# A conditioned decoder block on eight cores: x tiles in blocks and on another queue, the first squares summed on PE, the end by token halves

## The chip, the cores and the metric

The kernel runs on all eight cores of one Trainium2 chip. Each core computes one of eight sequences (4096 tokens of width 1024) with the same weights; the cores exchange nothing. The metric is the device time of the slowest core in microseconds (us). Engines are named as in the profile: PE is TensorE, DVE VectorE, ACT ScalarE, POOL GpSimd and SP SyncE. POOL and SP compute next to nothing here; they issue transfers, POOL on a queue whose descriptors are made in software (q0), SP on one with hardware descriptors (q1).

## The reference

The residual stream `x` (f32) goes through two feed-forward blocks (FFN) with a mixing block between, each behind an RMS norm that a conditioning vector `c` scales and shifts, and through a last such norm. Cut to what the change touches:

```python
D_MODEL = 1024; SEQ = 4096; D_FF = 2816
def rmsnorm(x, g):
    y = x * lax.rsqrt(jnp.mean(x * x, axis=-1, keepdims=True) + EPS)
    return y * g
def ada_rmsnorm(x, g, shift, scale):
    return rmsnorm(x, g) * (1.0 + scale) + shift
def swiglu_ffn(h, w_in, w_out):
    gate, up = jnp.split(h @ w_in, 2, axis=-1)
    return (jax.nn.silu(gate) * up) @ w_out

mod = silu(c) @ w_mod + b_mod                 # sh1, sc1, gt1, ... 9 vectors
h = ada_rmsnorm(x, g_ffn1, sh1, sc1)
x = x + 0.5 * gt1 * swiglu_ffn(h, w_ffn1_in, w_ffn1_out)
h = ada_rmsnorm(x, g_mix, sh2, sc2)
x = x + gt2 * (concat(conv_group(h), rglru_group(h)) @ w_out)
h = ada_rmsnorm(x, g_ffn2, sh3, sc3)
x = x + 0.5 * gt3 * swiglu_ffn(h, w_ffn2_in, w_ffn2_out)
return ada_rmsnorm(x, g_final, f_shift, f_scale)
```

## The kernel before

**Tiles.** The 4096 tokens of a core are eight tiles of T = 512. A tile is held with features on the partitions: eight blocks (`fc` 0 to 7) of 128 features by 512 tokens, f32, 2 MB in all, in one of four slots `xs` (sb_x). Its normalised copy in bf16 lies in one of three slots `hbs` (sb_hb). The hidden layer of an FFN (22 blocks of 128 by 512, bf16) is `hidA` or `hidB`.

**FFN.** The weights of an FFN are 33 slabs of 128 by 2048, read through a ring of five slots `fslots` (sb_fs). Slab `cg` below 22 holds 8 gate and 8 up blocks of one hidden block: 16 matmuls of 512 columns into two PSUM banks, then ACT takes the Silu of the gate bank into `sgf`, DVE multiplies with the up bank into the hidden layer (`evict`). The last 11 slabs are the output projection: for each of eight output blocks `oc` 22 matmuls into one bank, and DVE adds it, times the gate vector, into x (`oevict`). In its first use a slab comes as f32 from `w1` by POOL, which casts it on the way (`load_cast`), and SP writes it back in bf16 (`write_back`) for the later uses, which SP loads.

**Order of the work.** FFN 1 runs over pairs of tiles, (2, 3), (4, 5), (0, 1), then 6 and 7; the mixer and FFN 2 run over single tiles. The work is written as streams (generators), and `run_streams` interleaves them when the program is built, by a cost model. So each engine has a fixed list of instructions, which it carries out in order, with waits on semaphores between engines. A DMA's semaphore rises by 16.

**Head.** The modulation vectors come from 88 slabs of `wmod` (128 by 1024, f32, 512 KB). SP loads the first 16 at once (`modl_gen`) into buffers that are free then (sb_rs, sb_cs, sb_hidA, sb_hidB, sb_hb); DVE multiplies each with silu(c) and sums it (one SCALAR_TENSOR_TENSOR of 128x1024 into sb_junk, `mod_gen`), and every fourth frees a quarter of the first norm's scale and shift. Meanwhile POOL loads the first tile in one transfer (`xl_gen`, line 766), ACT squares its blocks, DVE adds the squares (`stats`, `accum`), one matmul with ones (`total`) sums over the partitions, ACT makes the reciprocal root by Ln and Exp (`rstd_ops`, sb_rstdm), and DVE and ACT apply it (`apply`). `head_gen` lets the first weight slab go when the ninth modulation slab is done, then the second x tile (one transfer on POOL, gated on the twelfth), then the others when the fifteenth is done.

**Between.** `o_gen` squares and sums x behind FFN 2 of a tile, applies the last norm and stores y in eight blocks on POOL, each with its own semaphore `s_y[fc]` (line 1284). The slot is then given to a later tile, whose eight block loads (`xload`) each wait for the store of the same block. In a pair or a mixer tile the statistics go by `stats` as above.

**End.** For the last tile the same: 8 x 22 matmuls of 512 columns, each output block squared and added as it comes, then the ones-matmul, Ln and Exp, eight DVE and ACT passes and eight stores.

## Time and profile before

| | us |
|---|---|
| median of three runs | 2373.75 |
| the three runs | 2369.35, 2373.75, 2509.9 |
| the profiled execution | 2375.25 |
| its span (first to last instruction), slowest core 7 | 2373.7 |
| the cores' spans | 2348.4 to 2373.7 |
| PE busy | 2249.8 (95%) |
| DVE busy | 1324.7 (56%) |
| ACT busy | 956.6 (40%) |
| POOL busy | 287.0 (12%) |

The profile is of one execution, of the slowest core. Busy time is what an engine spent inside instructions, its share is of the span. Matmuls overlap in the record (one of 512 columns is shown as some 380 ns while the next starts 217 ns after it), so a matmul's pace is read from the length of a run of them by their number. "Idle before" names what an engine waited for last. The granted clock is a share of TensorE's full 2.4 GHz; its lower level, 0.50, is 1.2 GHz.

### The profile page before, as it was taken

The page shows a single profiled execution, that of the slowest core. Times are in us where ns is not written, and L with a number is a line of the kernel's source. Part 1 is how long each engine was busy: PE and PEld are TensorE (multiplying, and loading weights), DVE is VectorE, ACT ScalarE, POOL GpSimd, SP SyncE. Part 2 cuts the span into 40 slices and gives each one's busy share as a digit, 9 for nine tenths or more (in the row PEclk, how much of TensorE's full clock was granted, in tenths as well). Part 3 has the DMA queues.
Part 4 walks back from the last instruction along what each step waited for, and adds up shares of the span by engine and source line. Part 5 has one row for each costly group of instructions (what it writes and reads, how often), then busy time and mean ns, then how long its engine had stood idle before and what let it go on. Part 6 is the DMA issues. An engine that isn't in the chain of part 4 may idle for free.

```text
span 2373.7 us, 34088 instructions; the slowest of 8 cores (2348.4 to 2373.7 us)
## 1 busy us (share of the span) xinstructions
PE 2249.8 (95%) x10864; PEld 1006.1 (42%) x10864; DVE 1324.7 (56%) x2131; ACT 956.6 (40%) x1473; POOL 287.0 (12%) x552
## 2 busy tenths in 40 slices
PE   1999998998999899899999999999999999999995
PEld 0444443443444344344444444444444444444442
DVE  5323225524433485674776476487487588477522
ACT  3313213303110533553565536436536556454512
POOL 0011110020000110201110120111111111120000
PEclk9999999999999999999999999999999999999998
DMA  9899798899866685654665665556456566564452
GB/s 258 189 232 215 194 206 214 214 212 243 214 187 164 191 223 170 190 167 141 194 207 158 207 200 191 154 171 227 153 178 214 160 171 222 158 186 138 151 177 89
DMA packets 122704, 446.86 MB, mean 188 GB/s; under 512 B 18864, under 2 KB 19248, under 8 KB 121520
## 3 DMA queue, kind: packets, MB, share of 16 engines
q1 hardware_dynamic: 90864, 330.44, 44.7%
q0 software_dynamic: 31664, 114.23, 21.5%
q8 instruction: 91, 1.49, 0.3%
q14 instruction: 85, 0.70, 0.1%
HBM read 426.87 MB, written 71.30 MB: 210 GB/s over the span
## 4 chain that ended last, share of the span: by engine, by line
PE 85%; DMA 8%; issue 2%; DVE 2%; ACT 2%; POOL 1%; SPq 0%; DVEq 0%; ACTq 0%; POOLq 0%
PE ps L457 83%; DMA sb_x<-x 2%; PE ps L1097 2%; DMA sb_cs<-wmod 2%; DMA sb_fs<-b 1%; DMA sb_fs<-w 1%; DMA sb_hidB<-wmod 1%; DMA sb_cs<-bm 1%; DVE sb_rstdm L441 1%; DMA x<-sb_x 0%; SPq L417 0%; POOL sb_urep L1087 0%; ACT sb_hb L434 0%; POOL sb_x L417 0%; ACT sb_ntmp L434 0%
## 5 line engine op out<-in xcount | busy, mean ns | idle before, releaser
L457 PE MATMUL ps<-sb_hb,sb_fs 128*128 128x512 bf16 x5632 | 1245.6, 382 | 35.5 <-DMA sb_fs<-w 14.2
L457 PEld LDWEIGHTS ps<-sb_hb,sb_fs 128*128 128x128 bf16 x5632 | 553.9, 98 | 711.8 <-issue 62.5
L457 PE MATMUL ps<-sb_hidA,sb_fs 128*128 128x512 bf16 x2288 | 505.7, 379 | 0.8 <-DVE sb_hidA L441 0.8
L434 ACT ACTIVATE sb_sgf<-ps 128x512 f32<-128x512 f32 x352 | 206.5, 593 | 406.8 <-PE ps L457 364.3
L457 PEld LDWEIGHTS ps<-sb_hidA,sb_fs 128*128 128x128 bf16 x2288 | 223.9, 98 | 269.6 <-issue 1.3
L441 DVE TENSOR_TENSOR sb_hidA<-ps,sb_sgf 128x512 bf16<-128x512 f32 x286 | 195.4, 688 | 227.1 <-PE ps L457 161.4
L457 PE MATMUL ps<-sb_hb,sb_cs 128*128 128x512 bf16 x992 | 224.2, 379 | 4.5 <-DMA sb_cs<-bm 3.4
L1087 POOL DMA_DIRECT2D sb_urep<-sb_ub x256 | 131.0, 520 | 694.5 <-PE ps L457 435.6
L437 DVE SCALAR_TENSOR_TENSOR sb_x<-ps,sb_gth,sb_x 128x512 f32<-128x512 f32 x128 | 96.0, 750 | 174.8 <-PE ps L457 174.4
L434 ACT ACT_TABLE_LOAD x102 | 130.9, 1283 | 154.4 <-PE ps L457 134.1
L437 DVE SCALAR_TENSOR_TENSOR sb_ux<-sb_ub,sb_vecs,sb_ux 128x512 f32<-128x512 bf16 x240 | 179.7, 749 | 10.0 <-DVE sb_ux L437 0.9
L434 ACT ACTIVATE sb_ntmp<-sb_x 128x512 f32<-128x512 f32 x168 | 103.6, 627 | 197.7 <-DVE sb_x L437 110.7
L441 DVE TENSOR_TENSOR sb_rstdm<-sb_rstdm,sb_ntmp 128x512 f32<-128x512 f32 x144 | 99.3, 689 | 131.5 <-ACT sb_ntmp L434 127.5
L437 DVE SCALAR_TENSOR_TENSOR sb_ntmp<-sb_x,sb_gs,sb_rstdm 128x512 f32<-128x512 f32 x192 | 137.8, 748 | 50.0 <-ACT sb_rstdm L434 41.7
L434 ACT ACTIVATE sb_hb<-sb_ntmp,sb_modv 128x512 bf16<-128x512 f32 x192 | 133.1, 720 | 43.1 <-DVE sb_ntmp L437 42.7
L457 PEld LDWEIGHTS ps<-sb_hb,sb_cs 128*128 128x128 bf16 x992 | 96.5, 98 | 122.3 <-issue 7.6
L457 PE MATMUL ps<-sb_hb,sb_rs 128*128 128x512 bf16 x544 | 128.8, 381 | 0.6 <-DVE sb_gy L437 0.4
L457 PE MATMUL ps<-sb_hidB,sb_fs 128*128 128x512 bf16 x528 | 117.9, 379 | 0.0
L441 DVE TENSOR_TENSOR sb_hidB<-ps,sb_sgf 128x512 bf16<-128x512 f32 x66 | 45.6, 691 | 109.5 <-PE ps L457 106.0
L417 POOL DMA_DIRECT2D y<-sb_x x64 | 35.0, 547 | 521.3 <-ACT sb_sgf L434 198.0
L437 DVE SCALAR_TENSOR_TENSOR sb_x<-ps,sb_modv,sb_x 128x512 f32<-128x512 f32 x64 | 47.9, 749 | 74.4 <-PE ps L457 74.3
L457 PEld LDWEIGHTS ps<-sb_hb,sb_rs 128*128 128x128 bf16 x544 | 53.4, 99 | 66.7 <-issue 4.1
(104 smaller groups left out, 1338.6 us busy)
## 6 DMA issues: line engine op xcount, KB each, us to landing
sb_fs<-b SPq DMA_DIRECT2D x396, 512.0 KB, 4.4
sb_cs<-bm SPq DMA_DIRECT2D x78, 512.0 KB, 4.1
sb_x<-x POOLq DMA_DIRECT2D x96, 256.0 KB, 7.9
sb_cs<-wmod SPq DMA_DIRECT2D x46, 512.0 KB, 12.6
sb_rs<-bm SPq DMA_DIRECT2D x34, 512.0 KB, 5.0
sb_fs<-w POOLq DMA_DIRECT2D x33, 512.0 KB, 9.9
b<-sb_fs SPq DMA_DIRECT2D x33, 512.0 KB, 8.8
b<-w POOLq DMA_DIRECT2D x33, 512.0 KB, 10.3
```

What stands on the lines that cost most here:

```text
L417: return Op(eng, lambda h: [h.dma_start(out=out_ap, in_=in_ap)], reads, writes, dma=sem, nbytes=nbytes)
L434: return Op(ACT, lambda h: [h.activation(out=out, in_=in_, func=func, **kw)], reads, writes, cost, tset)
L437: return Op(DVE, lambda h: [h.scalar_tensor_tensor(out=out, in0=in0, scalar=scalar, in1=in1, op0=op0, op1=op1)], reads, writes, cost)
L441: return Op(DVE, lambda h: [h.tensor_tensor(out=out, in0=in0, in1=in1, op=op)], reads, writes, cost)
L457: out.append(h.matmul(ps[:, bank, :], lhsT=l, rhs=r, start=(first and k == 0), stop=(last and k == n - 1)))
L1087: out.append(h.dma_start(out=urep[q][32 * sft:32 * sft + 32, 1 - h2:2, :], in_=ub[32 * q:32 * q + 32, 1 + h2:2 * h2 + 2, sft:sft + WU]))
L1097: out.append(h.matmul(ps[32 * q:32 * q + 32, b, :], lhsT=sl[:, 8 * (c % 2) + r, 32 * q:32 * q + 32], rhs=urep[q][:, c % 2, 4 * r:4 * r + T ...
```

## The change

It has four parts.

1. The first x tile is loaded as eight blocks on POOL's queue. The second is loaded as eight blocks on SP's queue, without a gate, behind the sixteen modulation slabs. The weight slabs are let go one by one, after modulation slab 8, 11 and 13 (indices 7, 10, 12) instead of 9 and 15.
2. The squares of the first tile are written as bf16, in two buffers by turns, and each is summed by a matmul with ones into one bank, instead of being added up on DVE. In the first tile's first slab of FFN 1 the gate and up matmuls alternate.
3. The output blocks 5 to 7 of the last tile's FFN 2 are computed in two halves of 256 tokens (`out_halves`), each with its own statistics, norm and stores (`o_half`), the stores on SP in pairs of blocks. An Exp of one column is put ahead of each half's Ln.
4. A tile's eight y stores share the semaphore `s_y[t % 4]`.

The functions for the convolution were also rewritten with the tables `CVD` and `CVP`; with the values given they make the instructions of before.

```diff
-        def xload(si, src, deps):
-            last = None
+        def xload(si, src, deps, eng=None, sem=None):
+            sem = sem or s_x[si]
             for fc in range(8):
-                op = dma(PL, xs[si][:, fc, :], src[:, fc, :], deps, [r_x[si][fc]], s_x[si], MB // 4)
+                op = dma(eng or PL, xs[si][:, fc, :], src[:, fc, :], deps, [r_x[si][fc]], sem, MB // 4)
                 yield op
...
-                    fplan.append(load_cast(w1_d[s], [r_start[min(s, 1)]]))
+                    fplan.append(load_cast(w1_d[s], [r_start[min(s, 2)]]))
...
-                    if gi == 0:
-                        yield dma(PL, xs[si][:], x_d[t], gate, r_x[si], s_x[si], 2 * MB)
+                    if t == groups[0][0]:
+                        yield from xload(si, x_d[t], [])
+                    elif gi == 0:
+                        yield lambda: mload[0] >= 16
+                        yield from xload(si, x_d[t], [], SP, newsem("s_xf"))
...
                     if first:
-                        yield lambda: mused[0] >= 5
-                    st = stat_m()
-                    yield from stats(xs[si], r_x[si], st)
...
+                        got = yield lambda: bankM.take(1)
+                        bank = got[0]
+                        for fc in range(8):
+                            sq, r_sq = ((sqb, r_sqb), (sqbo, r_sqbo))[fc % 2]
+                            yield act(sq[:], xs[si][:, fc, :], AF.Square, [r_x[si][fc]], [r_sq])
+                            yield mm(bank, [(ones_bf[:], sq[:])], [r_sq, r_ones], first=(fc == 0), last=(fc == 7))
...
-            for oc in range(8):
+            tail = xflag == "x3c" and g[0] == n_tiles - 1
+            for oc in range(OCF if tail else 8):
...
+        def out_halves(si, kb, freed, gth, r_gth):
...
+            for hf in range(2):
+                cols = slice(HT * hf, HT * hf + HT)
+                for oc in range(OCF, 8):
...
+                        yield mmh(b, prs, rr + r_hid[0][lo:hi_], lo == 0, hi_ == 22)
+                    yield stt(xs[si][:, oc, cols], ps[:, b, 0:HT], gth[:, oc:oc + 1], xs[si][:, oc, cols], ALU.mult, ALU.add,
+                              [r_bank[b], r_gth], [r_xh[hf][oc]], 0.45)
...
+        def o_half(hf):
...
+                    yield act(sgm[:, hf:hf + 1], hstate[:, 0:1], AF.Exp, [r_hst[0]], [r_sgm], tset="E", cost=0.2)
...
+            for fc in range(8):
+                yield stt(xt[:, fc, cols], xt[:, fc, cols], gsf[:, fc:fc + 1], acc, ALU.mult, ALU.mult, [r_acc, r_gsf], [r_xt[fc]], 0.45)
+                yield act(xt[:, fc, cols], xt[:, fc, cols], AF.Identity, [r_shf], [r_xt[fc]], bias=shf[:, fc:fc + 1], scale=1.0, cost=0.5)
+                if fc % 2 == 1:
+                    yield dma(SP, y_d[t, fc - 1:fc + 1, :, cols].rearrange("c p n -> p c n"), xt[:, fc - 1:fc + 1, cols], r_xt[fc - 1:fc + 1], [], s_yl, MB // 4)
...
-                    yield dma(PL, y_d[t, fc], xt[:, fc, :], [r_xt[fc]], [], s_y[fc], MB // 4)
+                    sy = s_y[t % 4]
+                    yield dma(PL, y_d[t, fc], xt[:, fc, :], [r_xt[fc]], [], sy, MB // 4)
+                for fc in range(8):
+                    r_xt[fc].r[sy] = sy.val
...
-            for j, kk in ((0, 8), (1, 14)):
+            for j, kk in ((0, 7), (1, 10), (2, 12)):
```

How the order moves, from the list of each engine's instructions. PE's list from its beginning, before (sb_ones with sb_sqb is a ones-matmul, sb_hb with sb_fs the FFN):

```order
L457 MATMUL ps<-sb_sqb,sb_ones 128x512
L457 MATMUL ps<-sb_hb,sb_fs 128x512 x32
L457 MATMUL ps<-sb_sqb,sb_ones 128x512
L457 MATMUL ps<-sb_hb,sb_fs 128x512 x592
L457 MATMUL ps<-sb_sqb,sb_ones 128x512
```

PE's list from its beginning, after:

```order
L460 MATMUL ps<-sb_sqb,sb_ones 128x512
L460 MATMUL ps<-sb_sqbo,sb_ones 128x512
L460 MATMUL ps<-sb_sqb,sb_ones 128x512
L460 MATMUL ps<-sb_sqbo,sb_ones 128x512
L460 MATMUL ps<-sb_sqb,sb_ones 128x512
L460 MATMUL ps<-sb_sqbo,sb_ones 128x512
L460 MATMUL ps<-sb_sqb,sb_ones 128x512
L460 MATMUL ps<-sb_sqbo,sb_ones 128x512
L460 MATMUL ps<-sb_hb,sb_fs 128x512 x12
L460 MATMUL ps<-sb_sqb,sb_ones 128x512
L460 MATMUL ps<-sb_hb,sb_fs 128x512 x612
```

One ones-matmul for the first tile became eight, and that of the second tile moved from behind 32 FFN matmuls to behind 12. POOL's list at the first x load into a slot whose y was stored, before, with the semaphores waited for:

```order
L417 DMA y<-sb_x 128x512 [waits s_act]
L417 DMA sb_x<-x 128x512 [waits s_y0]
L417 DMA sb_x<-x 128x512 [waits s_y1]
L417 DMA sb_x<-x 128x512 [waits s_y2]
L417 DMA sb_x<-x 128x512 [waits s_y3]
L417 DMA sb_x<-x 128x512 [waits s_y4]
L417 DMA sb_x<-x 128x512 [waits s_y5]
L417 DMA sb_x<-x 128x512 [waits s_y6]
L417 DMA sb_x<-x 128x512 [waits s_y7]
L417 DMA y<-sb_x 128x512 [waits s_act] x8
```

POOL's list at the same load and the next, after:

```order
L420 DMA y<-sb_x 128x512 [waits s_act]
L420 DMA sb_x<-x 128x512 [waits s_y0]
L420 DMA sb_x<-x 128x512 x7
L420 DMA y<-sb_x 128x512 [waits s_act] x8
L420 DMA sb_x<-x 128x512 [waits s_y1]
L420 DMA sb_x<-x 128x512 x7
```

The wait for the last of the eight stores stands now at the first of the eight loads; there are five such places. PE's list at its end, after (before it ends with 176 matmuls of 512 columns and one ones-matmul):

```order
L460 MATMUL ps<-sb_hidA,sb_fs 128x512 x110
L864 MATMUL ps<-sb_hidA,sb_fs 128x256 x58
L864 MATMUL ps<-sb_sqbo,sb_ones 128x256
L864 MATMUL ps<-sb_hidA,sb_fs 128x256 x22
L864 MATMUL ps<-sb_cvb,sb_ones 128x256
L864 MATMUL ps<-sb_hidA,sb_fs 128x256 x44
L864 MATMUL ps<-sb_sqb,sb_ones 128x256
L864 MATMUL ps<-sb_hidA,sb_fs 128x256 x8
L864 MATMUL ps<-sb_cvsq,sb_ones 128x256
```

66 matmuls of 512 columns became 132 of 256, with the first half's ones-matmul (sb_cvb) 58 matmuls ahead of the last. On SP the eight loads `sb_x<-x` stand between the sixteenth modulation slab and the first write-back, and eight y stores at the very end.

## Rows read from the trace of the kernel before

**Rows 1.** The page: busy time of PE; its commonest weight load

```profile
PE 2249.8 (95%) x10864; PEld 1006.1 (42%) x10864; DVE 1324.7 (56%) x2131; ACT 956.6 (40%) x1473; POOL 287.0 (12%) x552
...
L457 PEld LDWEIGHTS ps<-sb_hb,sb_fs 128*128 128x128 bf16 x5632 | 553.9, 98 | 711.8 <-issue 62.5
```

**Rows 2.** Timeline of PE, head: start us, us, what, xcount, idle before

```profile
43.70 2.72 PE L457 MATMUL ps<-sb_hb,sb_fs 128*128 128x512 bf16 x6 [10.07 <-DMA sb_fs<-w]
...
49.53 4.16 PE L457 MATMUL ps<-sb_hb,sb_fs 128*128 128x512 bf16 x10 [3.11 <-ACT sb_hb L434]
...
57.20 4.92 PE L457 MATMUL ps<-sb_hb,sb_fs 128*128 128x512 bf16 x16 [3.51 <-DMA sb_fs<-w]
...
62.83 11.82 PE L457 MATMUL ps<-sb_hb,sb_fs 128*128 128x512 bf16 x54
...
76.50 21.09 PE L457 MATMUL ps<-sb_hb,sb_fs 128*128 128x512 bf16 x97 [0.29 <-ACT sb_hb L434]
```

**Rows 3.** Timeline of the end, behind PE's last FFN matmul

```profile
2349.05 0.75 DVE L437 SCALAR_TENSOR_TENSOR sb_x<-ps,sb_gth,sb_x 128x512 f32<-128x512 f32 x1 [2.35 <-PE ps L457]
...
2352.10 1.28 ACT L434 ACT_TABLE_LOAD   x1 [1.52 <-PE ps L457]
...
2354.82 5.39 DVE L437 SCALAR_TENSOR_TENSOR sb_x<-sb_x,sb_gsf,sb_rstdo 128x512 f32<-128x512 f32 x8 [3.37 <-ACT sb_rstdo L434]
...
2356.94 5.18 POOL L417 DMA_DIRECT2D y<-sb_x  x8 [99.19 <-ACT sb_x L434]
```

**Rows 4.** Timeline of POOL at the first x load behind y stores

```profile
1193.20 3.73 POOL L417 DMA_DIRECT2D sb_x<-x  x7
1198.75 0.54 POOL L417 DMA_DIRECT2D sb_x<-x  x1 [1.82 <-DMA y<-sb_x]
```

**Rows 5.** Timeline of ACT, DVE and PE at x loads: first square, last addition, ones-matmul

```profile
1207.70 0.63 ACT L434 ACTIVATE sb_rstdm<-sb_x 128x512 f32<-128x512 f32 x1 [8.03 <-DMA sb_x<-x]
...
1218.37 0.38 PE L457 MATMUL ps<-sb_sqb,sb_ones 128*128 128x512 bf16 x1 [1.02 <-DVE sb_ub L449]
...
1332.11 0.68 DVE L441 TENSOR_TENSOR sb_sqb<-sb_rstdm,sb_ntmp 128x512 bf16<-128x512 f32 x1
...
1334.61 0.38 PE L457 MATMUL ps<-sb_sqb,sb_ones 128*128 128x512 bf16 x1
...
1468.87 0.38 PE L457 MATMUL ps<-sb_sqb,sb_ones 128*128 128x512 bf16 x1 [3.35 <-DVE sb_sqb L441]
...
1664.09 0.38 PE L457 MATMUL ps<-sb_sqb,sb_ones 128*128 128x512 bf16 x1 [0.67 <-DVE sb_sqb L441]
```

**Rows 6.** Timeline of ACT and DVE, head: tile 1, eighth slab, tile 2

```profile
16.29 0.63 ACT L434 ACTIVATE sb_rstdm<-sb_x 128x512 f32<-128x512 f32 x1 [4.85 <-DMA sb_x<-x]
...
28.68 1.22 DVE L656 SCALAR_TENSOR_TENSOR sb_junk<-sb_hidA,sb_cb 128x1024 bf16<-128x1024 f32 x1
...
54.44 0.63 ACT L434 ACTIVATE sb_rstdm<-sb_x 128x512 f32<-128x512 f32 x1 [1.69 <-DMA sb_x<-x]
...
61.78 0.69 DVE L441 TENSOR_TENSOR sb_sqb<-sb_rstdm,sb_ntmp 128x512 bf16<-128x512 f32 x1 [1.41 <-ACT sb_ntmp L434]
```

**Rows 7.** DMA: second tile's issue, to landing; queue q1 in 30:36; q0, q1 in 107:118

```profile
sb_x<-x POOLq DMA_DIRECT2D x1, 2048.0 KB, 13.1
...
q1 hardware_dynamic: 543, 1.98, 101.1%
...
q0 software_dynamic: 286, 1.04, 57.2%
q1 hardware_dynamic: 477, 1.74, 44.2%
```

**Rows 8.** Windows: us, PE, PEld, DVE, ACT, POOL busy, PEclk, DMA share, GB/s

```profile
1471.00:1473.00 2.00, 2.00 (x6) 0.76 (x5) 1.89 (x4) 1.97 (x3) 0.00 (x0) 0.50 0.00 0
```

**Rows 9.** The chain that ended last: a convolution of 32 matmuls

```profile
1964.08 1.84 PE ps L1097 x32
```

**Rows 10.** The stores y<-sb_x of the end (window 2340:2380)

```profile
DMA to landing us min/median/max: 2.3/3.0/3.3
```

More of the change, by code:

```diff
@@ L24 @@
 WU = 540
+CVD = (0,)
+CVP = (1, 2, 3)
 V_G1, V_GM, V_G2, V_GF = 0, 8, 16, 24
@@ L369, in build_program @@
         s_x1 = [newsem(f"s_xs{k}") for k in range(4)]
-        s_y = [newsem(f"s_y{k}") for k in range(8)]
+        s_y = [newsem(f"s_y{k}") for k in range(4)]
+        s_yl = newsem("s_yl")
         s_fs = [newsem(f"s_fs{k}") for k in range(NFS)]
@@ L812, in ffn_in @@
                 bg, bu = got
-                for half, b in ((0, bg), (8, bu)):
-                    if cg == 0:
-                        for kc in range(8):
-                            yield (lambda kc=kc: r_hb[hi][kc].w is not None)
+                if cg == 0:
+                    for kc in range(8):
+                        yield (lambda kc=kc: r_hb[hi][kc].w is not None)
+                        for half, b in ((0, bg), (8, bu)):
                             op = mm(b, [(sl[:, half + kc, :], hbs[hi][:, kc, :])], [r_sl, r_hb[hi][kc]], first=(kc == 0), last=(kc == 7))
                             yield op
-                    else:
+                else:
+                    for half, b in ((0, bg), (8, bu)):
                         op = mm(b, [(sl[:, half + kc, :], hbs[hi][:, kc, :]) for kc in range(8)], [r_sl] + r_hb[hi])
@@ L829, in ffn_in, with halves, mmh, fn @@
             flags.add(("fin", j))
+        HT = T // 2
+        OCF = 5
+        r_xh = []
+        r_oh = []
+        def halves(res):
+            out = []
+            for hf in range(2):
+                for r0 in res:
+                    r = Res()
+                    r.w = r0.w
+                    r.tw = r0.tw
+                    r.tr = r0.tr
+                    r.r = dict(r0.r)
+                    out.append(r)
+            n = len(res)
+            return [out[:n], out[n:]]
+        def mmh(bank, prs, reads, first, last):
+            n = len(prs)
+            def fn(h):
+                out = []
+                for k, (l, r) in enumerate(prs):
+                    out.append(h.matmul(ps[:, bank, 0:HT], lhsT=l, rhs=r, start=(first and k == 0), stop=(last and k == n - 1)))
+                return out
+            return Op(PE, fn, reads, [r_bank[bank]], 0.11 * n)
@@ new lines, in out_halves @@
+        def out_halves(si, kb, freed, gth, r_gth):
+            yield flag("o5")
+            r_xh.extend(halves(r_x[si]))
+            r_oh.extend(halves([r_ro]))
+            for hf in range(2):
+                streams.append(Stream(f"O{hf}", o_half(hf), b_m))
+            for hf in range(2):
+                cols = slice(HT * hf, HT * hf + HT)
+                for oc in range(OCF, 8):
+                    got = yield lambda: bankF.take(1)
+                    b = got[0]
+                    for lo, hi_ in ((0, 14), (14, 22)):
+                        prs = []
+                        rr = []
+                        for k in range(lo, hi_):
+                            idx = oc * 22 + k
+                            sk = kb + idx // 16
+                            yield fring.has(sk)
+                            sl, r_sl = fring.at(sk)
+                            prs.append((sl[:, idx % 16, :], hids[0][:, k, cols]))
+                            if r_sl not in rr:
+                                rr.append(r_sl)
+                        yield mmh(b, prs, rr + r_hid[0][lo:hi_], lo == 0, hi_ == 22)
+                    yield stt(xs[si][:, oc, cols], ps[:, b, 0:HT], gth[:, oc:oc + 1], xs[si][:, oc, cols], ALU.mult, ALU.add,
+                              [r_bank[b], r_gth], [r_xh[hf][oc]], 0.45)
+                    bankF.give(b)
+                    flags.add(("x3h", oc, hf))
+            while freed < kb + NF1 - FC:
+                fring.done(freed)
+                freed += 1
@@ L921, in ffn @@
             yield from oevict(oev)
+            if tail:
+                yield from out_halves(x_of(g[0]), kb, freed, gth, r_gth)
         def tick(op, phase1):
@@ L1086, in fn @@
                     for sft in range(4):
[L1087 to L1088 removed]
+                        out.append(h.dma_start(out=urep[q][32 * sft:32 * sft + 32, c0 - 2 * h2:2, :],
+                                               in_=ub[32 * q:32 * q + 32, c0:2 * h2 + 2, sft:sft + WU]))
                 return out
[L1090 removed]
+            return Op(PL, fn, [r_ub[k] for k in range(c0, 2 * h2 + 2)], [r_urep], dma=s_ur, nbytes=128 * 4 * (2 * h2 + 2 - c0) * WU * 2, ndma=16)
         def conv_mm(b, sl, r_sl, c):
@@ L1127, in c_gen @@
                 bankM.give(bv)
-                if c == 0:
-                    streams.append(Stream(f"V{i}", v_gen(i), dict(b_m, dve=0)))
-                if c == 1:
+                if c in CVD:
+                    streams.append(Stream(f"V{i}.{c}", v_gen(i, c), b_v))
+                if c == 1 and CVP[0] < 2:
                     yield spread(0)
             flags.add(("glu", i))
-            for c in range(1, 4):
+            for c in CVP:
+                if c == 2 and CVP[0] == 2:
+                    yield cring.has(k0 + 4)
+                    cring.done(k0 + 4)
+                    yield spread(1)
                 k = k0 + 4 + c // 2
@@ L1273, in o_gen @@
                 st = stat_o()
+                if t == n_tiles - 1:
+                    for fc in range(OCF):
+                        yield flag(("x3c", t, fc))
+                        yield from accum(st, xt[:, fc, :], r_xt[fc])
+                    flags.add("o5")
+                    return
                 yield from stats(xt, r_xt, st, before=lambda fc, t=t: flag(("x3c", t, fc)))
```

102 lines of the change are left out of this document (65 added, 37 removed).

## The prediction

> **What bounds the kernel now.** I read the page first: PE is busy 95% of the span [rows 1], so a change pays or costs only where PE stands still, at the head, at the end, and at a few waits between. Then the timeline of each such place. The order in which the program's instructions stand (it is fixed when the kernel is built) shows that the change alters three places and leaves the rest as it was.
>
> At the head PE's real work starts at 43.70 us and comes in pieces until 76.50, from where it runs on; the idle time ends first on a weight slab (10.07 us, then 3.51), then on the normalised tile [rows 2]. By 76.50 PE has done 6 + 10 + 16 + 54 + 1 = 87 FFN matmuls. That count at that time is my yardstick for the head. At the end the reader is to see a chain without PE: the last accumulation is read at 2349.05, an activation table is loaded (1.28 us), eight DVE passes of 512 tokens follow, ACT's behind them, and eight stores [rows 3]. In between, x tiles are loaded into slots from which y has just been stored, and ACT and PE wait for them [rows 4, 5].
>
> **First tile in blocks.** One 2 MB transfer becomes eight of 256 KB on the same queue; all eight have one semaphore and ACT waits for the full count. Seven such issues took 3.73 us [rows 4], so the last leaves 4 us after the first. Before, ACT starts on x at 16.29; DVE, which works through the modulation slabs, reaches its eighth only at 28.68 [rows 6], and the first use of the reciprocal root now stands behind that eighth. Eight squares with a matmul each, at some 0.75 us, need 6 us: ready at about 25. That is 4 us of cover, and the blocks cost nothing while they land within it. The seven additions that leave DVE (0.69 us each, as at 61.78 [rows 6]) save little, since DVE then waits for slabs: 0.
>
> The Trainium skill speaks against the blocks: DMA: Bandwidth & Descriptors, section Rules for kernel authors, wants at least 1 MiB per DMA. The trace bears on it by the second tile, which as one transfer took 13.1 us for 2 MB [rows 7]; eight blocks took 14.5 us from the first issue to ACT's start, 1.8 us of waiting among them [rows 4, 5]. So the trace shows no price for the blocks; by the rule the first tile would come later, which its 4 us of cover hide in part, and by the rows it doesn't.
>
> **Second tile behind the slabs.** This is the term that I size largest at the head. Two things move together. First, in PE's order the ones-matmul of the second tile's squares now stands after 12 FFN matmuls instead of 32. So 75 of the 87 stand behind the landing of the second tile plus its statistics. Second, that tile is now last in SyncE's queue, while the weight slabs (cast transfers) start earlier on GpSimd's. SyncE's queue alone moves 1.98 MB in 6 us, 0.33 MB/us; beside the casts it moves 1.74 MB in 11 us, 0.158 MB/us [rows 7]. The eighth slab is worked on at 28.68; at 1.6 us a slab about 4.6 slabs are left at 33 us, when the first cast begins to flow. With the 2.1 MB of x that is 4.5 MB. At 0.158 they take 28 us, less some 3 us in which no cast flows: x is there at about 58 us, against 54.44 before, where ACT starts on it [rows 6]. From there to the ones-matmul it took 8.0 us (54.44 to 61.78 plus 0.69), with two evictions in between that are now gone; I take 7: 65 us. The 75 matmuls take 75 x 0.217 (21.09/97 [rows 2]) = 16.3 us, plus 1.4 because after an idle time the first 16 took 4.92 instead of 3.5 us: 82.7 against 76.50. **Head: +6 us.** Bounds: with 0.33 MB/us all the way x lands at about 47 and the statistics start at 50, when ACT is free of the first tile: 57 + 17.7 = 74.7, -2. With the casts taking still more, x at 64: +12. That the weights come earlier helps nothing, as no slab is waited for once x is the last to come. The write-backs of the slabs now queue behind x on SyncE; their slots are needed again only after 80 us.
>
> **Fewer store semaphores.** The eight stores of a y tile now share one semaphore, and the next x load into that slot waits, at its first block, for all eight. Before, seven loads went out at once (1193.20) and only the eighth waited for the eighth store (1198.75) [rows 4]. Now the first goes out when the eighth went before, and the last some 3.9 us later. ACT started 8.9 us after the last issue (1207.70 [rows 5]), so it starts up to 3.9 us later; I take 3.5, since the store lands sooner without loads beside it. Behind the waiting load on GpSimd stand its seven fellows and, later, copies for the convolution, which have tens of us of room. There are five such places. At the first, PE runs the ones-matmul at 1218.37 right behind its operands and has waited 1.02 us: all 3.5 are PE's. At the second DVE is done at 1332.79 and PE comes at 1334.61: 1.8 of slack, 1.7 left. At the third PE already waits 0.67: 3.5. At the fourth and fifth ACT does not wait for x today, and I take 0. An idle time of such a length also slows what follows: after one of 3.35 us [rows 5] two microseconds at a granted clock of 0.50, the lower level of 1.2 GHz, held 6 matmuls instead of 9 [rows 8]; some 4 us like that cost 1.4. Sum 8.7 + 2.5, less about 2 for small waits that stand in the same stretches and are swallowed. **Middle: +9 us.** Bounds: 2 if the stores land at once and PE's slack is larger on the slowest core, 16 with full delays at all five and a slow clock behind each.
>
> **End by halves.** PE does 110 matmuls of 512 columns, then 132 of 256. No row shows one of 256 columns with a full weight load. Bounds: half of 0.217 each (nothing lost), or 0.217 each (+14.3 us). The convolution's 32 matmuls take 1.84 us, 0.058 us for a matmul with its own load [rows 9], so the pair can be issued faster than 0.108; I take half. After PE's end the path was 2349.05 to 2362.12 (last store issued) plus 2.3 to 3.3 to land [rows 10]; with 2.4 (2364.5) that is 15.6 us from PE's last matmul, which ends 0.1 before 2349.05. Now for the second half: accumulate 0.5, square 0.5, ones-matmul 0.4, two activations that wait for the first half's last passes 1.5, eight DVE passes of half length at 0.4 instead of 0.67 = 3.2, ACT's last 0.6, issue 0.4, landing 2.5: 9.5. The table load is out of the way, as an Exp of one column pulls it under PE's work. Against this stand three small matmuls and two short waits in PE's stream, 0.7. **End: 9.5 + 0.7 - 15.6 = -5.4**; I take -5. What follows the last landing (2364.5 to the end of the span) is the same for both.
>
> The Trainium skill, TensorE: Matmul & The Clock Gate, section Back-to-back issue gap, lists 262 cycles for 256 columns, 109 ns, but says that in a stream of weight loads and matmuls both set the pace (81 instead of 56 ns at 128 columns). An estimate by that rule would put 25 ns on each of the 132, 3.3 us. No row here shows it, and the convolution's row speaks against it.
>
> **Sum.** +6 + 9 - 5 = +10. The profiled execution took 2375.25 us (span 2373.7), the median of the three runs shown is 2373.75, 1.5 less. That gives 2384; I shade it to 2383, as the slowest core changes from run to run and a delay may fall on one that has room.
>
> **Rivals.** (a) Gain: x lands at 50 or before (the hardware queue keeps its 0.33 MB/us beside casts), so the head gives -2; the late loads cost 3; the end gives -5: 2370. For it: in the stretch of 107 to 118 us SyncE's queue may not have had work all the time, so 0.158 can be too low. Against: the shares of both queues sum to about one there. (b) Slower: half matmuls cost as much as whole ones because the weight load no longer fits under the stream. PE's end moves by 14.3: 2397. It decides from the first of the 132 on, and the price grows with each ns above 108; at 0.15 us it eats the end's gain. For it: a load is shown as 98 ns busy [rows 1]. Against: the convolution's 0.058 [rows 9]. (c) The change does not do what it says: squares on PE and blocks free DVE and bring x no earlier, as DVE waits for slabs. The first part of that is in the forecast; if the other terms came to nothing as well, the time would stay at 2374, inside the range.
>
> **How the numbers follow.** Forecast (slightly slower, 2374 to 2395) 0.55; (a) 0.32; (b) 0.10; 0.03 for what I have not seen. The range of eight in ten takes in (a) and cuts (b): 2364 to 2398. Two per cent (about what a measurement of this kernel can tell from no change) are 47 us, and no case reaches them; 0.02 on each side.
>
> **What would show it.** In the changed profile: PE's 87th FFN matmul at 83 us, the second tile's first square at 58; at the first load behind stores one idle time of GpSimd before eight loads instead of before the last, and ACT on x 3.5 us later after it, with PE's waits for the ones-matmul grown from about 1 us to 4; 132 matmuls of 256 columns in 14.3 us; 9 to 10 us from PE's last matmul to the last landing. I am wrong if x lands at 50, if PE's waits behind the x loads do not grow, or if the half matmuls run at 0.13 or more.

## The result and the profile after

The changed kernel is slower by one per cent. Its median was 2398.76 us over 7 runs, against 2374.85 us for the kernel before beside it; the ratio is 1.0102, 95% interval 1.0078 to 1.0126, about 24 us. The forecast was 2383.0 us with a range of 2364 to 2398: the sign was right, the size less than half of what came, and the range was missed by a little.

Single runs scatter by more than the effects below, since the slowest of eight cores is another one each time. So beside the ratio I give a second number: the mean span of all cores, over all runs, of this kernel minus that of the kernel before on the same chip, with its 95% interval. Cores of a die whose clock was disturbed (below 0.978 in the records) are left out of it.

First, the page of the changed kernel, busy time: to compare with [rows 1].

```profile
PE 2260.3 (94%) x10940; PEld 1015.3 (42%) x10940; DVE 1321.5 (55%) x2136; ACT 955.3 (40%) x1486; POOL 286.6 (12%) x550
```

PE is busy 10.5 us longer in a span 23.5 us longer. So more than half of the loss is PE standing still. The timeline of PE at the head shows the greatest part of it in one line (columns as in [rows 2]).

```profile
41.85 5.18 PE L460 MATMUL ps<-sb_hb,sb_fs 128*128 128x512 bf16 x12 [10.31 <-DMA sb_fs<-w]
72.56 0.59 PE L460 MATMUL ps<-sb_sqb,sb_ones 128*128 128x512 bf16 x1 [25.52 <-DVE sb_sqb L444]
72.94 27.47 PE L460 MATMUL ps<-sb_hb,sb_fs 128*128 128x512 bf16 x116
```

PE does twelve FFN matmuls and then stands still for 25.5 us, since the next instruction in its order is the second tile's ones-matmul. That matmul waits for the statistics, and these wait for the second tile, which comes eleven microseconds later than in [rows 6]. Timeline of ACT (first and second tile) and of SyncE's queue:

```profile
25.17 0.63 ACT L437 ACTIVATE sb_sqb<-sb_x 128x512 bf16<-128x512 f32 x1 [13.19 <-DMA sb_x<-x]
...
65.62 0.63 ACT L437 ACTIVATE sb_rstdm<-sb_x 128x512 f32<-128x512 f32 x1 [14.53 <-DMA sb_x<-x]
...
25.68 15.26 SPq L420 DMA_DIRECT2D sb_x<-x  x8
```

The other cores show the same: over the eight cores the second tile's first square stands at a median of 63.5, against 53.1 before. The 87th FFN matmul, my yardstick, is the 75th behind the ones-matmul. From 72.94, 75 x 0.213 and 2.7 for the slow start of that row give about 91.6, against 76.50.

In the middle, the first x load behind y stores (timelines of POOL, ACT, PE; compare [rows 4, 5]), then the third and the fifth such place; ACT's lines are of the third, the fourth and the fifth.

```profile
1211.50 4.53 POOL L420 DMA_DIRECT2D sb_x<-x  x8 [5.46 <-DMA y<-sb_x]
...
1663.93 4.24 POOL L420 DMA_DIRECT2D sb_x<-x  x8 [4.16 <-DMA y<-sb_x]
...
1999.73 4.46 POOL L420 DMA_DIRECT2D sb_x<-x  x8 [5.66 <-DMA y<-sb_x]
...
1677.66 0.63 ACT L437 ACTIVATE sb_rstdm<-sb_x 128x512 f32<-128x512 f32 x1 [6.04 <-DMA sb_x<-x]
...
1846.57 0.63 ACT L437 ACTIVATE sb_rstdm<-sb_x 128x512 f32<-128x512 f32 x1 [2.33 <-DMA sb_x<-x]
...
2014.71 0.63 ACT L437 ACTIVATE sb_rstdm<-sb_x 128x512 f32<-128x512 f32 x1 [4.28 <-DMA sb_x<-x]
...
1685.63 0.58 PE L460 MATMUL ps<-sb_sqb,sb_ones 128*128 128x512 bf16 x1 [4.41 <-DVE sb_sqb L444]
```

As forecast, one wait now stands before all eight loads, where it stood before the last. But ACT waits for x at the fourth and the fifth place too, where it did not before.

At the end, PE's half matmuls and the two last passes, on PE, DVE and SyncE's queue; against [rows 3].

```profile
2362.57 6.50 PE L864 MATMUL ps<-sb_hidA,sb_fs 128*128 128x256 bf16 x58
...
2377.56 1.03 PE L864 MATMUL ps<-sb_hidA,sb_fs 128*128 128x256 bf16 x8
...
2381.45 3.25 DVE L440 SCALAR_TENSOR_TENSOR sb_x<-sb_x,sb_gsf,sb_rstdo 128x256 f32<-128x256 f32 x8 [1.48 <-ACT sb_rstdo L437]
...
2375.27 10.50 SPq L420 DMA_DIRECT2D y<-sb_x  x8
```

And the same matmuls as a group (busy time, then mean ns of one; the mean is of overlapping matmuls, so the pace is in the busy time):

```profile
L864 PE MATMUL ps<-sb_hidA,sb_fs 128*128 128x256 bf16 x132 | 15.0, 272 | 0.0
```

132 in 15.0 us are 0.114 each. PE's last FFN matmul ends at 2378.6, the last store is issued at 2385.4 and its kind lands in 2.2 us or a little more, near 2388: 9 to 10 us, where the kernel before took 15.6.

### The profile page after: what moved, and what is told of

It is laid out like the page before. It is cut to its first block, busy times and chain, and to the rows that moved or that the text cites. A ratio compares the mean times of both kernels' runs of the same rounds, so it can differ in the third digit from the quotient of the medians.

```text
span 2397.2 us, 34257 instructions; the slowest of 8 cores (2371.7 to 2397.2 us)
## 1 busy us (share of the span) xinstructions
PE 2260.3 (94%) x10940; PEld 1015.3 (42%) x10940; DVE 1321.5 (55%) x2136; ACT 955.3 (40%) x1486; POOL 286.6 (12%) x550
## 4 chain that ended last, share of the span: by engine, by line
PE 82%; DMA 9%; issue 2%; DVE 2%; ACT 2%; SPq 1%; POOL 1%; DVEq 0%; ACTq 0%; POOLq 0%
PE ps L460 80%; DMA sb_x<-x 5%; PE ps L1204 1%; DMA sb_fs<-b 1%; SPq L420 1%; POOL sb_x L420 1%; DVE sb_rstdm L444 1%; DMA x<-sb_x 1%; DMA y<-sb_x 1%; PE ps L864 1%; DMA sb_cs<-bm 0%; ACT sb_ntmp L437 0%; DMA sb_fs<-w 0%; POOL sb_urep L1194 0%; ACT sb_sgf L437 0%
## 5 line engine op out<-in xcount | busy, mean ns | idle before, releaser
L460 PE MATMUL ps<-sb_hidA,sb_fs 128*128 128x512 bf16 x2222 | 491.5, 379 | 0.8 <-DVE sb_hidA L444 0.8
L460 PEld LDWEIGHTS ps<-sb_hidA,sb_fs 128*128 128x128 bf16 x2222 | 217.4, 98 | 261.9 <-issue 1.3
L440 DVE SCALAR_TENSOR_TENSOR sb_x<-ps,sb_gth,sb_x 128x512 f32<-128x512 f32 (+1 forms) x131 | 96.6, 738 | 179.4 <-PE ps L460 173.8
L437 ACT ACTIVATE sb_ntmp<-sb_x 128x512 f32<-128x512 f32 (+1 forms) x163 | 100.0, 623 | 182.7 <-DVE sb_x L440 109.9
L460 PE MATMUL ps<-sb_sqb,sb_ones 128*128 128x512 bf16 x27 | 12.0, 444 | 81.8 <-DVE sb_sqb L444 53.5
## 6 DMA issues: line engine op xcount, KB each, us to landing
sb_cs<-wmod SPq DMA_DIRECT2D x46, 512.0 KB, 10.5
```

The lines of the kernel that those rows point to most:

```text
L437: return Op(ACT, lambda h: [h.activation(out=out, in_=in_, func=func, **kw)], reads, writes, cost, tset)
L440: return Op(DVE, lambda h: [h.scalar_tensor_tensor(out=out, in0=in0, scalar=scalar, in1=in1, op0=op0, op1=op1)], reads, writes, cost)
L460: out.append(h.matmul(ps[:, bank, :], lhsT=l, rhs=r, start=(first and k == 0), stop=(last and k == n - 1)))
```

## The experiments

Three terms stand in the forecast: head, middle, end. The first four runs take them apart. The experiments ran in four batches, each on one chip (e1 to e4, e5 to e8, e9 to e12, e13 to e15). A difference between kernels of two batches goes over the kernel before, which ran on every chip, and is uncertain by 2.5 to 3 us.

**One thing put back, or one alone.** e1_sem8 is the changed kernel with this edit:

```diff
-        s_y = [newsem(f"s_y{k}") for k in range(4)]
+        s_y = [newsem(f"s_y{k}") for k in range(8)]
...
-                    sy = s_y[t % 4]
+                    sy = s_y[fc]
...
-                for fc in range(8):
-                    r_xt[fc].r[sy] = sy.val
```

> The changed kernel with one semaphore per feature block for the y stores, as before the change, instead of one for all eight blocks of a tile; nothing else, and the order on every engine is the changed kernel's. Theory (shared store semaphore costs about 14 us in the middle): 10 to 14 us less than the changed kernel, so about +10 us against the kernel before (ratio 1.004); the wait on y in front of each first x load goes back to a 1.8 us one ahead of the eighth, and ACT's waits for x shrink by about 3 us each. Rival (the middle's loss follows from the head's or from the clock): less than 4 us gained, ratio 1.009 or more.

Measured: ratio 1.0015 (0.9974 to 1.0055), mean core +8.9 ± 1.8 us against before.

e2_oldhead puts back the head of before (its transfers, gates, squares on VectorE, matmul order) and keeps shared semaphores and the new end.

> The changed kernel with the whole head of before (both first tiles as one 2 MB transfer each on GpSimd's queue, the second gated on the twelfth modulation slab, squares of the first tile summed on VectorE, the cast loads' gates and the first matmuls' order of before). Theory (the new head costs 14 us): ones-matmul of the second tile back at about 61.8, its 87th FFN matmul at 76 to 77, and 14 us less than the changed kernel (ratio 1.004 against before). Rival (the first 50 us are caught up by slack later, because PE then waits at about 98 and 540 for weight slabs anyway): 4 us or less gained.

Measured: ratio 1.0041 (1.0006 to 1.0075), mean core +11.2 ± 2.0.

e3_both makes both edits. What is left of the change is the end by halves.

> The kernel before with the end by token halves alone: old head, eight store semaphores for tiles 0 to 6. Theory (the three terms add: head +14, shared semaphore +14, end -5): about 5 us faster than before, ratio 0.998, 9 to 10 us from PE's last FFN matmul to the last landing. Rival (half-width matmuls cost PE at once what they save, or the changed placement of the last tile moves a wait elsewhere): 0 to +3 us, ratio 1.000 or more.

Measured: ratio 0.9981 (0.9937 to 1.0025), mean core -5.5 ± 1.4.

e4_before_shared is the kernel before with the reverse of the diff above.

> The kernel before with one edit, one store semaphore for all eight blocks of a tile; the order on every engine is that of before. Theory: +10 to +15 us (ratio 1.004 to 1.006), a wait of about 5 us before the first of eight x loads at the places of y stores. Rival (the waits show on GpSimd, but a slack of 4 us per tile hides them): +3 us or less, ratio under 1.0015.

Measured: ratio 1.0029 (0.9981 to 1.0076), mean core +16.6 ± 2.0.

All four ran on one chip. The shared semaphore is found twice: it costs 16.6 by e4, and 16.7 as e2 minus e3. The head costs 14.4 (e1 minus e3). The end gives 5.5. The sum is 25.5. The whole change was measured at 24 on the slowest core; by the mean core, the measure of the parts, the changed kernel's 2384.4 stands against 2361.6 in the one profiled execution beside it and 2362 to 2366 on the four chips of the experiments, so 18 to 23. The parts add up to that or to a little more. The theories of e1, e2 and e3 held about as forecast. That of e4 held in kind, but its 16.6 lies above its 10 to 15. None of the four rivals held. All of this rests on the mean core: by the ratio alone e1, e3 and e4 are not told from no change.

**How the shared semaphore costs more than forecast.** Timeline of e4, POOL and ACT at the second place, then ACT at the fourth and fifth:

```profile
1311.05 0.54 POOL L417 DMA_DIRECT2D y<-sb_x  x1 [1.17 <-ACT sb_x L434]
1316.15 2.13 POOL L417 DMA_DIRECT2D sb_x<-x  x4 [4.56 <-DMA y<-sb_x]
1318.49 2.12 POOL L417 DMA_DIRECT2D sb_x<-x  x4 [0.21 <-issue]
...
1331.81 0.63 ACT L434 ACTIVATE sb_rstdm<-sb_x 128x512 f32<-128x512 f32 x1 [7.77 <-DMA sb_x<-x]
...
1841.01 0.63 ACT L434 ACTIVATE sb_rstdm<-sb_x 128x512 f32<-128x512 f32 x1 [5.32 <-DMA sb_x<-x]
...
2006.91 0.63 ACT L434 ACTIVATE sb_rstdm<-sb_x 128x512 f32<-128x512 f32 x1 [2.89 <-DMA sb_x<-x]
```

The time from the issue of the last y store to ACT's first square is the number to read. In the kernel before it is 15.1, 14.4 and 14.8 us at the first three places; in e4 18.8, 20.8 and 19.9. That is 3.7, 6.4 and 5.0 later, not 3.5. (In the changed kernel it is 19.7, 18.0 and 18.4: 4.6, 3.7 and 3.6 later.) At the fourth and fifth place the kernel before shows no wait, and 17.5 and 16.7 us from that store to the square. If the data needs some 14.8 there too, it had been there for 2.7 and 1.9 us. By this estimate that is all the slack there was. In e4 the two squares come 23.0 and 19.7 us after the store, so the delay goes through it.

e8_before_two is the kernel before with two semaphores for each tile (blocks 0 to 3, blocks 4 to 7). Its edit is shown against e4_before_shared; the list has eight semaphores again:

```diff
-                    sy = s_y[t % 4]
+                    sy = s_y[2 * (t % 4) + fc // 4]
```

> The kernel before with two store semaphores per tile, one for blocks 0 to 3 and one for 4 to 7; order on every engine that of before. In e4_before_shared the last of eight x loads was issued about 10 us after the last store, before the change about 6; with two semaphores 7.5 to 8. Theory (the cost goes by how late the loads end): 40 to 50% of the cost of one semaphore, 7 to 8 us more than before (ratio 1.003). Rival (the cost goes by the first load, which now waits for nothing): 0 to 2 us. Rival (any load that waits for the last store costs the whole): 15 us.

Measured: ratio 0.9996 (0.9971 to 1.0022), mean core +1.6 ± 2.3. The first rival was right, though not by its reason. Timeline of e8, POOL and ACT at the first place:

```profile
1201.45 0.59 POOL L417 DMA_DIRECT2D y<-sb_x  x1
1202.03 2.14 POOL L417 DMA_DIRECT2D sb_x<-x  x4
1207.55 2.12 POOL L417 DMA_DIRECT2D sb_x<-x  x4 [3.37 <-DMA y<-sb_x]
...
1216.47 0.63 ACT L434 ACTIVATE sb_rstdm<-sb_x 128x512 f32<-128x512 f32 x1 [7.97 <-DMA sb_x<-x]
```

From last store to square it is 15.0 here, and 14.8 and 14.7 at the next two places: as with eight semaphores, though the last load is issued 1.6 us later. The last load still counts, as ACT waits for all eight. But with half of the tile already under way ACT starts sooner after its issue (7.3 us, against 8.9), which makes up for the later issue here.

**What in the head costs.** Five runs start from e1_sem8 and put back one thing. e5_x2pool puts the second tile back as one 2 MB transfer on GpSimd's queue, with the gates of before:

```diff
-                        yield lambda: mload[0] >= 16
-                        yield from xload(si, x_d[t], [], SP, newsem("s_xf"))
+                        yield flag("x1go")
+                        yield lambda: r_modr[order[11]].w is not None
+                        yield dma(PL, xs[si][:], x_d[t], [r_modr[order[11]]], r_x[si], s_x[si], 2 * MB)
```

> The changed kernel with eight store semaphores (as e1_sem8) and, in its head, only the second tile and the cast loads' gates put back: one 2 MB transfer on GpSimd's queue behind the twelfth modulation slab. First tile in blocks, its squares summed on PE and the new matmul order stay. Theory (the head's loss is the late second tile): 12 to 15 us less than e1_sem8, about 5 us faster than before (ratio 0.998), second tile's ones-matmul near 62 with 32 FFN matmuls ahead of it. Rival (the first tile's blocks, which land 9 us later than the one transfer, or the squares on PE, are part of the loss): 5 to 10 us less than e1_sem8, ratio 1.000 to 1.002.

Measured: ratio 0.9964 (0.9944 to 0.9984), mean core -7.0 ± 1.7. The theory holds: 15.9 less than e1, so the first tile's part costs nothing that shows. By a third of a per cent it is faster than the kernel before.

e6_late2 and e7_late4 leave the transfers and alter PE's order alone (2 or 4 column groups of 16 matmuls each):

```diff
                         yield from stats(xs[si], r_x[si], st)
+                        if t == groups[0][1]:
+                            yield lambda: ahead[0] >= 2
```

> e1_sem8 with one edit: the second tile's ones-matmul is held back in PE's order until 32 of the first tile's FFN matmuls stand ahead of it, as before the change, instead of 12. The second tile itself still lands behind the modulation slabs. Theory (two losses in the head: the tile lands 11 us later, and PE has 20 matmuls fewer to fill the wait): about 4.3 us (20 x 0.213) less than e1_sem8, PE idle some 21 instead of 25.5 us in front of that ones-matmul. Rival (only the landing counts, the work moved ahead is wanted later at once): within 1 us of e1_sem8.

Measured: ratio 1.0026 (1.0003 to 1.0049), mean core +2.5 ± 2.1, 6.4 less than e1_sem8. The theory holds for the time. PE's idle time before that ones-matmul was expected at 21 us and fell further, from 25.5 to 16.0:

```profile
50.85 6.47 PE L460 MATMUL ps<-sb_hb,sb_fs 128*128 128x512 bf16 x20 [2.19 <-ACT sb_hb L437]
73.30 0.59 PE L460 MATMUL ps<-sb_sqb,sb_ones 128*128 128x512 bf16 x1 [15.99 <-DVE sb_sqb L444]
```

The 20 matmuls brought a wait of their own, and they took 6.47 us there, not 4.3. So the shorter idle time is not all gain.

> As e6_late2 with 64 matmuls of the first tile ahead of the second tile's ones-matmul. Theory (idle PE time filled by work that is ready): 52 matmuls, 11 us, move into the wait, 3 to 4 us come back as waits for the second tile's first hb blocks, so 6 to 8 us less than e1_sem8, and about 2 us more than before in all. Rival (as in e6_late2, or the third and fourth weight slabs land too late for it): 4 us or less.

Measured: ratio 1.0026 (1.0005 to 1.0047), mean core +3.9 ± 2.6, 5.0 less than e1_sem8. The theory (6 to 8) was too high, and the scatter does not tell it from e6. The next lines of PE's timeline in e7 show where it went:

```profile
52.36 12.13 PE L460 MATMUL ps<-sb_hb,sb_fs 128*128 128x512 bf16 x47 [0.44 <-DMA sb_fs<-w]
73.31 0.59 PE L460 MATMUL ps<-sb_sqb,sb_ones 128*128 128x512 bf16 x1 [8.82 <-ACT sb_sgf L437]
74.10 6.29 PE L460 MATMUL ps<-sb_hb,sb_fs 128*128 128x512 bf16 x16 [0.21 <-DVE sb_hidA L444]
80.64 1.09 PE L460 MATMUL ps<-sb_hb,sb_fs 128*128 128x512 bf16 x4 [0.26 <-ACT sb_hb L437]
82.88 1.25 PE L460 MATMUL ps<-sb_hb,sb_fs 128*128 128x512 bf16 x4 [1.14 <-ACT sb_hb L437]
```

The matmuls moved ahead do fill the wait. But then the first tile's slabs are used up, and PE waits piece by piece for the second tile's hb. Work can be moved ahead of a late tile only until that tile is the only thing left.

e9_x2pool_gates has the second tile as in e5, but the cast loads' gates of the changed kernel.

> e5_x2pool with the changed kernel's gates for the cast loads (8th, 11th and 13th modulation slab) instead of those of before; the second tile is still one transfer on GpSimd's queue behind the twelfth slab, now after two weight slabs instead of one, and its ones-matmul stands behind 48 FFN matmuls. Theory (PE's head is bound by the bytes that must land, so an order of the same bytes gives back what it takes): first weight slab some 4 us and second some 5 us earlier, second tile some 3 us later, in all within 2 us of e5_x2pool. Rival (earlier weight slabs let PE start earlier for good): 4 us less than e5_x2pool. Rival (part of the changed head's loss was the gates): 3 us or more above e5_x2pool.

Measured: ratio 0.9985 (0.9963 to 1.0007), mean core -4.8 ± 2.1. That is 2.2 more than e5, within 2.7 either way: the first rival (4 less) is out, but between the theory (within 2) and the second rival (3 or more above) this run does not decide. PE starts at 42.4 instead of 45.7 and waits longer afterwards.

e10_x1_one is e5 with the first tile as one transfer, e11_oldend is e5 with the old end.

> e5_x2pool with the first tile in one 2 MB transfer instead of eight blocks; squares still summed on PE. Theory (rstd of the first tile waits for nothing on the critical path, since the apply waits for modulation slabs and the first FFN matmul for its weight slab): first square at about 16 instead of 25, time within 1.5 us of e5_x2pool. Rival (the blocks keep the queue busy, slabs and weights land later): 2 to 4 us less than e5_x2pool.

Measured: ratio 0.9968 (0.9951 to 0.9986), mean core -7.9 ± 2.2. The first square moved to 16.08, and the second tile's from a median of 53.5 to 50.0. The time did not move beyond the scatter.

> e5_x2pool with the last tile's end as before the change (all eight output blocks full width, y on GpSimd's queue): what is left of the change is the first tile in blocks with its squares on PE. Theory (end worth 5.4 us, first tile worth nothing): 5 us more than e5_x2pool, within 1.5 us of before (ratio 0.999 to 1.001). Rival (the first tile's part gives something of its own): 2 us or more less than before, ratio 0.999 or less.

Measured: ratio 1.0000 (0.9981 to 1.0020), mean core -2.6 ± 1.7. It is 4.4 above e5, near the end's 5.5. The two numbers leave open whether the first tile's part is worth nothing or two microseconds.

**The form of the transfer.** e12_x2sp_one leaves the second tile at its new place, last on SyncE's queue, and changes only its form:

```diff
-                        yield from xload(si, x_d[t], [], SP, newsem("s_xf"))
+                        yield dma(SP, xs[si][:], x_d[t], [], r_x[si], newsem("s_xf"), 2 * MB)
```

> e1_sem8 with the second tile as one 2 MB transfer on SyncE's queue behind the sixteen modulation slabs, instead of eight blocks of 256 KB there. Theory (late because it stands behind the slabs): the tile lands within 2 us of e1_sem8's, second ones-matmul at 71 to 73, time within 2 us of e1_sem8. Rival (late because eight small transfers take SyncE's queue 15 us to issue and each moves slowly): lands 5 us or more earlier, 5 us or more less than e1_sem8.

Measured: ratio 0.9992 (0.9973 to 1.0012), mean core -1.6 ± 1.7, that is 10.5 less than e1_sem8. The theory fell and the rival was right: the second tile's first square came at a median of 55.7 over the cores instead of 63.4. The place behind the slabs was the small part of the trouble; the eight blocks were the large one. Here are the DMA queues from 41 to 56 us (packets, MB, share of the 16 engines' time), first e1_sem8:

```profile
q0 software_dynamic: 372, 1.38, 53.4%
q1 hardware_dynamic: 901, 1.96, 46.8%
```

and e12_x2sp_one:

```profile
q1 hardware_dynamic: 411, 2.96, 56.7%
q0 software_dynamic: 308, 1.10, 45.3%
```

q0 carries the casts, q1 the last of the modulation slabs and the second tile. In both kernels each holds about half of the engines' time. In that half q1 moves 2.2 KB a packet as blocks and 7.2 KB as one transfer: 1.96 against 2.96 MB. These are the slowest cores; the medians of the eight are 1.82 and 2.54 MB. The Trainium skill, DMA: Bandwidth & Descriptors, section Rules for kernel authors, asks for at least 1 MiB per DMA. This trace agrees: as one transfer of 2 MB the tile came 7.7 us earlier than as eight of 256 KB.

Is it the number of transfers, or the size of their rows? e13_x2_rows cuts the tile in eight by partitions, so that rows stay at 16 KB:

```diff
+                        for k in range(8):
+                            p = slice(16 * k, 16 * k + 16)
+                            yield dma(SP, xs[si][p], x_d[t][p], [], [r_x[si][k]], sxf, MB // 4)
```

> e12_x2sp_one with the second tile in eight transfers of 256 KB again, but cut by partitions (16 rows of 16 KB each) instead of by feature blocks (128 rows of 2 KB each). Theory (the size of the packets decides: 41:56 us both queues hold about half of the DMA engines' time in either kernel, and with 2.2 KB a packet SyncE's moved 1.96 MB, with 7.2 KB 2.96 MB): lands at 56 to 58 as in e12_x2sp_one, first square of the second tile there. Rival (the number of transfers decides: fixed cost of each, SyncE's queue filled): lands at 62 to 66 as in e1_sem8.

Measured: ratio 1.0033 (1.0018 to 1.0048), mean core +4.9 ± 2.3; first square at a median of 60.7. e14_x2_two uses two transfers of four blocks.

> e12_x2sp_one with the second tile in two transfers of 1 MB (four feature blocks, 8 KB a row). Theory (packet size, with little left to gain above some KB): lands at 56 to 59. Rival (number of transfers, 1.2 us each): 57 to 58, which this run can't tell apart; but if it lands at 61 or later both are wrong and the place in the queue or the casts beside it matter more.

Measured: ratio 0.9995 (0.9984 to 1.0007), mean core +0.5 ± 1.4; first square at a median of 58.8. So neither explanation holds alone. The medians stand in the order 63.4 (eight, 2 KB rows), 60.7 (eight, 16 KB rows), 58.8 (two, 8 KB rows), 55.7 (one, 16 KB rows). The longer rows give 2.7 us with the count fixed at eight, and going from eight to one gives 5.0 with the rows fixed at 16 KB. Each median is of one execution: e6 and e7, whose transfers in the head are those of e1, have 65.6 and 64.9, so the 2.7 is uncertain by some 2. One reservation more: a transfer of 16 rows was slower for each packet. From 41 to 56 us q1 of e13 took

```profile
q1 hardware_dynamic: 424, 2.59, 78.8%
```

which is 78.8% of 16 x 15 us for 424 packets, 0.45 us each, against 0.33 in e12 (medians of the eight cores 0.59 and 0.36). So part of the 5.0 may belong to the cut by partitions. How much was not tried. Nor did the two queues share the time evenly here: q0 had 28.7%.

**Put together.** e15_best is e12 with the first tile as one transfer too and the edit of e6.

> e12_x2sp_one (eight store semaphores, end by halves, second tile as one transfer behind the slabs on SyncE's queue) with the first tile as one transfer too and 32 FFN matmuls ahead of the second tile's ones-matmul. Theory: x lands at 53 to 55, ones-matmul at 60 to 62, PE's head 3 to 4 us better than before the change, with the end's 5: 8 to 9 us faster than before, ratio 0.9965. Rival (the first tile and the slabs share the engines, the second tile gains nothing): like e10_x1_one or e3_both, 5 to 7 us faster than before.

Measured: ratio 0.9962 (0.9938 to 0.9987), mean core -6.4 ± 1.5, median 2367.67 us: faster than both kernels. The mean core has the size that its rival gave (5 to 7); the ratio 0.9962 would be 9 us, the theory's size, and its interval holds both. Its head is 0.9 better than that of before (-6.4 against e3's -5.5), which the scatter does not tell from nothing. e5, e10 and e15 come out alike, each a third of a per cent faster than the kernel before, and the end by halves is most of it.

## Why the prediction was right in sign and short in size

**First tile in blocks: 0, and so it was, by a wrong reading.** I held that the trace showed no price for blocks, by loads in the middle. At the head, beside the modulation slabs, the blocks landed nine microseconds later than the one transfer (25.17 against 16.29). The cover hid it nearly whole: DVE waited 1.8 us for the reciprocal root, and e10 moved the landing back without a gain.

**Head: +6 forecast, 14.4 measured.** The step that failed is "x is there at about 58 us". It came at 65.6 on the slowest core. The arithmetic behind it took 0.158 MB/us for SyncE's queue beside the casts, from [rows 7], and that row is of other transfers: 1.74 MB in 477 packets, 3.6 KB each. It was also the highest of the eight cores in that window (the others moved 1.29 to 1.61 MB). The blocks of x have shorter rows, and from 41 to 56 us the queue moved 1.96 MB in e1, 0.131 MB/us; over the changed kernel's cores the median is 1.78 MB, 0.119. With 0.131 my sum would have given 64, which I had only as the outer bound (+12). I had weighed the Trainium skill's rule on large transfers (page and section as above) and applied it to the first tile, where a cover stood, and not to the second, which had none. e12 shows what that was worth: 10.5 ± 2.5 of the 14.4. The other part, that 75 instead of 55 FFN matmuls stand behind the landing, was seen rightly. It was worth some 4 us by its own count of 20 x 0.213, and e6 recovered 6.4 ± 2.8.

**Middle: +9 forecast, 16.6 measured.** The mechanism was right: one wait before eight loads, and ACT later by the store's landing. The step that failed is "at the fourth and fifth ACT does not wait for x today, and I take 0"; two sizes besides were short. The delay of ACT was taken as 3.5 and measured in e4 as 3.7, 6.4 and 5.0 at the first three places. At the fourth and fifth the ones-matmuls of e4 stand another 2.3 and 2.4 us later. A place without a wait has slack of unknown size, and I took it for enough. It could have been read: 17.5 and 16.7 us from store to square, against the 14.8 that the other places need. The slow clock was there as forecast, but larger: in e4 the shift grows from 11.8 at the third place's ones-matmul (1664.09 to 1675.88) to 13.8 at the next (1711.65 to 1725.46), with no wait between. Behind the second place 56 FFN matmuls took 13.65 us instead of 12.25, behind the first eight took 3.42 instead of 1.89. That is some 4.9 in all, where I had taken 2.5:

```profile
1675.88 0.59 PE L457 MATMUL ps<-sb_sqb,sb_ones 128*128 128x512 bf16 x1 [5.64 <-DVE sb_sqb L441]
...
1725.46 0.38 PE L457 MATMUL ps<-sb_sqb,sb_ones 128*128 128x512 bf16 x1
```

The 2 us that I subtracted for swallowed waits came as well. PE's waits for weight slabs behind the first place and behind the fifth shrank or went, and the shift fell by 1.2 and 1.3 us. First the kernel before, then e4:

```profile
1283.68 3.61 PE L457 MATMUL ps<-sb_hb,sb_cs 128*128 128x512 bf16 x16 [1.48 <-DMA sb_cs<-bm]
...
2040.09 3.61 PE L457 MATMUL ps<-sb_hb,sb_cs 128*128 128x512 bf16 x16 [1.11 <-DMA sb_cs<-bm]
...
1284.65 3.61 PE L457 MATMUL ps<-sb_hb,sb_cs 128*128 128x512 bf16 x16 [0.74 <-DMA sb_cs<-bm]
```

The 16.6 ± 2.0 lie at the bound of 16 that I gave for full delays at all five places. Delays at all five places came, those at the last two about half as large. These shifts compare the slowest core of one execution with that of another.

**End: -5 forecast, 5.5 measured.** Every step came out: 9 to 10 us from PE's last matmul to the last landing, and 132 half matmuls in 15.0 us instead of 14.3. Rival (b) is out. Part of this was luck: the row that I held against (b), the convolution's 0.058, is of weight loads of 32 columns (128*32), not of full ones, and said nothing of them. By the estimate from the Trainium skill, TensorE: Matmul & The Clock Gate, section Back-to-back issue gap, each would have taken 25 ns more; the trace shows 6 ns.

**The rivals.** (a) needed x at 50; it came at 65, on the other side of my number. (c) was half true: the squares on PE and the first tile's blocks brought nothing that could be told. Head and middle have one error in common: a size was carried over from a row of another kind of transfer or place, and both times in the friendlier direction.

## What to carry to other kernels

A rate read from one queue's row holds for that row's transfers, and for that core: look at the others too. Beside the casts, eight transfers with short rows moved fewer bytes in the same share of the engines' time (1.82 against 2.54 MB in 15 us) than one large one. Where a semaphore is shared, ask which of the waits becomes the first one: a half-tile semaphore cost nothing here that could be measured, a whole-tile one 16.6 us. A place where nothing waits is not free; measure its slack by a like place that does wait.

## What the runs showed that I had not expected

The form of the second tile's transfer, same bytes, same queue and same place in it, moved its landing by 7.7 us and the kernel by 10.5 ± 2.5: eight transfers of 256 KB against one of 2 MB. And the mean granted clock, 0.983 in the changed kernel and 0.988 before, is more a sign of the loss than its cause, as the low values belong largely to PE's idle time. In the changed kernel's window from 60 to 72 us (columns as in [rows 8])

```profile
60.00:72.00 12.00, 0.00 (x0) 0.00 (x0) 4.43 (x7) 4.82 (x8) 0.00 (x0) 0.50 0.65 240
```

PE did nothing, and the clock stood at 0.50, the level of 1.2 GHz. From 47 to 60 it was 0.62 and from 72 to 76 0.50. In the kernel before it was 0.87 from 47 to 60 and 1.00 in the other two. By these numbers the three stretches make some 0.005 of the mean over the span (an estimate), which is about the whole difference. The price is in the first matmuls afterwards, as in [rows 8]: the convolution's 32 matmuls of [rows 9] took 3.53 us instead of 1.84 behind a wait:

```profile
1227.69 3.53 PE L1204 MATMUL ps<-sb_urep,sb_cs 128*32 128x512 bf16 x32 [2.00 <-DVE sb_hidA L444]
```
